# A table of score offsets kept in device memory as 128 copies of its strips instead of one, and read forwards instead of backwards

## The reference

```
bias_band = rel_bias[t5_bucket(dist[0])]                      # rel_bias: 32 buckets x 16 heads
s_band = einsum(q, k) * scale + bias_band
s_band = where((k_pos >= BLOCK) & (dist >= 0) & (dist < WINDOW), s_band, NEG)
bias_m = rel_bias[t5_bucket(dist_m)]                          # query against the 16 meta tokens
s_meta = where(dist_m >= 0, einsum(q, k_meta) * scale + bias_m, NEG)
p = softmax(concatenate([s_meta, s_band, sink]))
```

## Time and profile before

| | |
|---|---|
| median of 3 runs | 1749.38 us (1748.59 to 1753.09) |
| the profiled execution | 1753.09 us, its span 1751.3 us |
| PE busy | 1667.7 us, 95% of the span |
| DVE, ACT, POOL busy | 59%, 52%, 12% |
| bytes moved | 266.00 MB, of which POOL's queue 3.28 MB |
| TensorE clock granted | 0.986 of full speed on average |

### The profile page before, as it was taken

How to read it: one execution, slowest core, us unless ns; L and a number is a source line. 1 busy time by engine, 2 the same in 40 slices (tenths; PEclk the granted TensorE clock), 3 DMA queues, 4 the chain that set the end, 5 groups by cost and what they waited for, 6 DMA issues and landing times.

```text
span 1751.3 us, 31633 instructions
## 1 busy us (share of the span) xinstructions
PE 1667.7 (95%) x12915; PEld 1596.3 (91%) x12915; DVE 1033.4 (59%) x2139; ACT 911.5 (52%) x2008; POOL 217.5 (12%) x257
## 2 busy tenths in 40 slices
PE   8999999999999999999899997999977989999997
PEld 7999999899997999999889996988976769999997
DVE  5555566655555655554565554544366876768863
ACT  4444354644436544465465444566743447556653
POOL 4000000000000000001100000345433551200000
PEclk9999999999999999999999999999989999999999
DMA  8555535365554555643346554633351224645551
GB/s 276 175 169 175 182 125 172 122 190 169 177 178 131 169 179 180 194 131 114 121 144 190 177 187 120 176 113 104 113 154 60 78 69 136 201 145 177 179 181 43
DMA packets 260207, 266.00 MB, mean 152 GB/s; under 512 B 4755, under 2 KB 259025, under 8 KB 260064
## 3 DMA queue, kind: packets, MB, share of 16 engines
q1 hardware_dynamic: 258528, 260.72, 47.3%
q0 software_dynamic: 1536, 3.28, 0.8%
HBM read 262.89 MB, written 1.09 MB: 151 GB/s over the span
## 4 chain that ended last, share of the span: by engine, by line
PE 84%; issue 4%; ACT 4%; DVE 3%; POOL 3%; DMA 0%; SPq 0%; DVEq 0%; POOLq 0%; ACTq 0%
PE ps L803 51%; PE ps L805 25%; POOL EX L1911 2%; PE ps L516 1%; ACT wh L1137 1%; PE ps L772 1%; POOL YB L1939 1%; PE ps L615 1%; POOL EX L1912 0%; ACT H L918 0%; DVE BC L1684 0%; DVE wl L1626 0%; POOL wl L1947 0%; ACT XH L913 0%; PE ps L752 0%
## 5 line engine op out<-in xcount | busy, mean ns | idle before, releaser
L1626 DVE TENSOR_TENSOR wl<-raw,wh 128x512 fp32r<-128x512 f32 x923 | 609.9, 713 | 395.2 <-ACT wh L1137 386.7
L1137 ACT ACTIVATE wh<-raw 128x512 fp32r<-128x512 f32 (+1 forms) x989 | 548.2, 620 | 213.7 <-PE ps L803 212.9
L803 PE MATMUL ps<-XH,wh 128*128 128x272 f32 (+2 forms) x2264 | 577.5, 291 | 16.0 <-ACT XH L913 6.7
L805 PE MATMUL ps<-XH,wl 128*128 128x272 f32 (+2 forms) x2264 | 568.9, 287 | 0.0
L803 PEld LDWEIGHTS ps<-XH,wh 128*128 128x128 f32 x2264 | 431.2, 190 | 21.6 <-issue 14.7
L805 PEld LDWEIGHTS ps<-XH,wl 128*128 128x128 f32 x2264 | 432.5, 191 | 0.2
L803 PE MATMUL ps<-XL,wh 128*128 128x272 f32 (+2 forms) x2264 | 310.6, 288 | 0.2 <-DVE XL L1407 0.2
L803 PEld LDWEIGHTS ps<-XL,wh 128*128 128x128 f32 x2264 | 290.0, 189 | 4.2 <-DVE XL L1407 2.8
L803 PE MATMUL ps<-HH,wh 128*128 128x272 f32 (+1 forms) x704 | 173.1, 284 | 0.0
L805 PE MATMUL ps<-HH,wl 128*128 128x272 f32 (+1 forms) x704 | 173.1, 284 | 0.0
L803 PEld LDWEIGHTS ps<-HH,wh 128*128 128x128 f32 x704 | 132.5, 188 | 0.0
(11 more groups left out here) (363 smaller groups left out, 2022.2 us busy)
## 6 DMA issues: line engine op xcount, KB each, us to landing
raw<-in_ffn_wg SPq DMA_DIRECT2D x44, 1024.0 KB, 5.4
raw<-in_ffn_wu SPq DMA_DIRECT2D x44, 1024.0 KB, 5.4
raw<-in_w_in SPq DMA_DIRECT2D x33, 1024.0 KB, 5.4
raw<-in_ffn_wd SPq DMA_DIRECT2D x32, 1024.0 KB, 5.2
raw<-in_w_ffn_in SPq DMA_DIRECT2D x22, 1024.0 KB, 5.1
raw<-in_ffn_wd SPq DMA_DIRECT2D x16, 768.0 KB, 4.8
raw<-in_conv_w_in SPq DMA_DIRECT2D x12, 1024.0 KB, 5.1
raw<-in_kv_w SPq DMA_DIRECT2D x8, 1024.0 KB, 5.4
```

The source lines that it names most:

```text
L803: mm = e.matmul(o, hi[:, k, c], xk, start=u.first and part == 0 and k == 0, stop=u.last and end)
L805: e.matmul(o, lo[:, k, c], xk, start=False, stop=False)
L1137: e.activation(wh[u.n % NH][:, c], raw[u.n % NR][:, c], ACT.Copy).then_inc(s_hi, 1)
L1626: e.tensor_tensor(wl[u.n % NH][:, c], raw[u.n % NR][:, c], wh[u.n % NH][:, c].bitcast(F32), ALU.subtract).then_inc(s_lo, 1)
```

## The change

The scratch tensor grows from 16 x 672 numbers (43 KB) to 128 x 16 x 672 numbers (5.5 MB). One transfer still writes it, from the same 16 partitions, but its source is repeated 128 times, so each head's row of 2688 bytes is written 128 times, 43,008 bytes apart. The constants are built in the opposite order (the strips unreversed, and the strip of the window ahead of that of the meta tokens). The reads have the same shapes as before. Partition q now reads in copy q of the strips, at an offset that falls by 4 bytes from one q to the next; so the keys come out in rising order, and DVE adds the rows forwards. Number, order and shapes of all instructions on all engines stay as they were; the two parts of `B2` change places (16 and 256 columns).

```diff
-    db, dm = 255 - np.arange(STRIP)[::-1], 271 - np.arange(MSTRIP)[::-1]
-    both = np.concatenate([dm, db])
+    db, dm = 255 - np.arange(STRIP), 271 - np.arange(MSTRIP)
+    both = np.concatenate([db, dm])
...
-            e.tensor_tensor(SS[:, 0:272], PS[4][:, 0:T], B2[:, h, ::-1], ALU.add).then_inc(s_s2, 1)
+            e.tensor_tensor(SS[:, 0:272], PS[4][:, 0:T], B2[:, h, :], ALU.add).then_inc(s_s2, 1)
             e.wait_ge(s_sc1, 8 + h + 1)
-            e.tensor_tensor(SS[:, 272:288], PS[5][:, 0:16], B1[:, h, ::-1], ALU.add)
-            e.tensor_tensor(SS[:, 288:416], PS[5][:, 16:144], B2[:, h, 127::-1], ALU.add).then_inc(s_s1, 1)
-            e.tensor_tensor(SS[0:16, 416:432], PS[5][0:16, 144:160], B0[:, h, ::-1], ALU.add).then_inc(s_s0, 1)
+            e.tensor_tensor(SS[:, 272:288], PS[5][:, 0:16], B1[:, h, :], ALU.add)
+            e.tensor_tensor(SS[:, 288:416], PS[5][:, 16:144], B2[:, h, 144:272], ALU.add).then_inc(s_s1, 1)
+            e.tensor_tensor(SS[0:16, 416:432], PS[5][0:16, 144:160], B0[:, h, :], ALU.add).then_inc(s_s0, 1)
...
         e.wait_ge(s_smk, 1)
-        e.dma_start(scratch, SMK).then_inc(s_b, 16)
+        e.dma_start(scratch.rearrange("q h j -> h q j"),
+                    SMK.unsqueeze(1).to_broadcast([16, 128, WS])).then_inc(s_b, 16)
...
-        sk, sv = A["attn_sinks_2"], scratch
+        sk, sv, pitch = A["attn_sinks_2"], scratch, 16 * WS
 
         def shifted(off, nq, n):
-            return bass.AP(tensor=sv.tensor, offset=sv.offset + WS - n - off, ap=[[1, nq], [WS, 16], [1, n]])
+            return bass.AP(tensor=sv.tensor, offset=sv.offset + off, ap=[[pitch - 1, nq], [WS, 16], [1, n]])
...
-        e.dma_start(B2[:, :, 0:256], shifted(127, 128, 256)).then_inc(s_b, 16)
-        e.dma_start(B2[:, :, 256:272], shifted(STRIP + 271 - 144, 128, 16)).then_inc(s_b, 16)
+        e.dma_start(B2[:, :, 16:272], shifted(127, 128, 256)).then_inc(s_b, 16)
+        e.dma_start(B2[:, :, 0:16], shifted(STRIP + 271 - 144, 128, 16)).then_inc(s_b, 16)
...
-    scratch = nc.dram_tensor("strips", (16, STRIP + MSTRIP), F32, kind="Internal").ap()
+    scratch = nc.dram_tensor("strips", (128, 16, STRIP + MSTRIP), F32, kind="Internal").ap()
```

More of the change, by code:

```diff
@@ L43, in bucket @@
         return np.where(d < 16, d, np.minimum(big, 31))
-    db, dm = 255 - np.arange(STRIP)[::-1], 271 - np.arange(MSTRIP)[::-1]
-    both = np.concatenate([dm, db])
+    db, dm = 255 - np.arange(STRIP), 271 - np.arange(MSTRIP)
+    both = np.concatenate([db, dm])
     hot = (bucket(both)[None, :] == np.arange(32)[:, None]).astype(np.float32)
-    ok = np.concatenate([dm >= 0, (db >= 0) & (db < 128)])
+    ok = np.concatenate([(db >= 0) & (db < 128), dm >= 0])
     smask = np.broadcast_to(np.where(ok, 0.0, NEG).astype(np.float32), (16, both.size))
```

## The result

| | before | after |
|---|---|---|
| median | 1750.17 us (4 runs, 1748.59 to 1753.09) | 1780.51 us (4 runs, 1778.31 to 1784.07) |
| the profiled execution | 1753.09 us, span 1751.3 | 1777.53 us, span 1775.7 |
| POOL's queue | 3.28 MB | 8.74 MB |

The ratio is 1.018, with a 95% interval of 1.0164 to 1.0198 (it goes by all 21 executions of the changed kernel, the table's median by four of them): some 30 us slower. The forecast was 1771, in a range of 1748 to 1784.

The account below looks back on a forecast made before the run. The prediction took PE to bound the kernel around the write, with weights 24 us ahead; 19.2 us for late weights plus 2.0 for the clock, 21.2 on the median of 1749.38, gave 1771 us, range 1748 to 1784.

Parts of the forecast that it names:

- What bounds, and the lead: Around the strips' write PE has no gap, 634 to 694 us; the weight stream runs 24 us ahead of it.
- G: Gate weight unit SP issues at 636.88, after the write; PE late only if it lands after 666.1; forecast to land at 668.
- as long as the write less 24 us: Sign during the write: if PE's gap has this length, the mechanism stands even if the write took another time.
- The rate of the source: The 5.5 MB write from 16 partitions goes at 101 GB/s, taking 54.5 us, from 635.7 to 690.2.
- What the weights get: During the write: some 5 us without any, then one 1 KB packet per row; PE 19.2 us late.
- U: Up weight unit SP issues at 642.80; forecast to land near 691, with PE starting on it at 692.2 instead of 673.0.
- The clock: After PE's standstill of some 17 us, a granted clock of 0.50 costs 2.0 us; bounds 0 and 3.
- The wait of the residual: DVE's first residual waits for the write to land; it moves to about 715, so the write is in time, no cost.
- The reads: POOL's reads from 1100 us, same shapes with addresses 43 KB apart: taken as 0, bounds 0 and up to 12 us.
- a rival allowed: Rival: reads get faster without 128 partitions reading one 43 KB copy; at most 1 us, 1748; 0.02 for over 5 us.
- a hidden write: Rival: the 16 partitions don't limit the write, so both weight units land in time; 1749 to 1752 us, chance 0.31.
- weights that pass it: Rival: the write is slow, but engines fetch weights while a row's source keeps them waiting; 1749 us, chance 0.06.

## Why the prediction was right, and where it wasn't

- **What bounds, and the lead.** Right. G was to be needed at 666.1, with the stage's shift of 0.89 at 667.0. It landed at 693.2, 26.2 us late, and the gap is 26.6. With half the bytes it landed at 668.0, 1.9 us late, and the gap is 2.3. Two numbers beside it were wrong. A write of 36 us as the point where the loss begins: one of 30.5 us already had a gap. And the sign "as long as the write less 24 us": that is 32.7, not 26.6, since G is issued 2.1 us after the write and takes 5.4 us in any case. It comes out in G's landing time: 55.4 - 5.4 - 24 = 26.0.
- **The rate of the source.** Right: 101 GB/s was taken from a 0.4 us window, and the write ended at 692.3 where 690.2 was forecast. Since the window holds little (15 records of 2688 bytes, not all 16 rows), that it came out so near is partly luck. The 0.21 us a row of the same group, by which the write would have been hidden, was misleading: it was taken with one row for each engine, and over the whole write an engine needs 56.7/128 = 0.44 us for a row.
- **What the weights get.** Right in kind, mis-sized. The prediction took a row for a packet, and 5 us without any weights. It was two rows, and some 15 us without any. So G, forecast at 668, landed at 693, and it is G that PE waited for, not U. The term was 19.2, measured 26.6, too small by 7.4 us. The case that the prediction named beside its sum ("if the weights got nothing at all", 27 us) has nearly the number, but it isn't what happened: 0.72 MB of weights passed up to 690, and the write ended 2.1 us later and G landed 0.9 us behind it instead of 3.1. The trace of before could have told both. In the earlier trace rows 0.77 MB in 198 packets is four rows of 1 KB each, so a packet isn't a row. And from 1100 to 1108 POOL's queue had passed 355 packets, 1.33 MB, before the weights got their first.
- **The clock.** Right: in the window 695:700, at 0.50, PE issues 25 matmuls for 44, which is 2.2 us lost; it had started at 694.74, and the gap leaves 2.6 of the 29.2 us. Forecast 2.0.
- **The sum and the range.** 21.2 us were forecast, 26.6 + 2.6 = 29.2 arose. The measured 1780.51 lies within 1748 to 1784, but the upper end stood for something else, a write of 68 us. The write was as forecast, and the late weights took the time up there.
- **The wait of the residual.** Never met: DVE's first residual came at 724.30, 32 us after the write.
- **The reads.** They got faster, which a rival allowed: 10.7 us instead of 13.3. In 2 us in which POOL's queue is alone it moves 0.72 MB (1134:1136 of the kernel after) instead of 0.47. No gain can be told from it, as that rival's own bound of 1 us said: the run with 128 source partitions has these reads and no gap, at a ratio of 0.9993 (0.9977 to 1.0009).
- **DVE's forward reads.** 438 ns for 437. Nothing.
- **The rivals.** Those of a hidden write and of weights that pass it fell, by the gap. The first comes true with 128 source partitions: 19.1 us, no gap.

No version beats the kernel before: the changed kernel with the write from 128 partitions is level with it.

## What to carry to other kernels

Before adding a transfer beside a prefetch stream, work out two numbers: how long the transfer keeps the DMA engines (its bytes over what its narrow side allows, here 106 GB/s for 16 partitions against 400 for 128), and how far ahead the stream is. Measure it at the landing of the first load that is issued behind the transfer: in every run with the write on POOL's queue this load landed after the write's end, by 3 us at most. Weights that were late by less than the lead cost nothing here, beyond it each us was paid in full. Spreading the source over 128 partitions hid all of the 30 us (ratio 0.9993). Half the bytes from 16 partitions still cost 4 us in its trace, too little for the times to tell. The transfer cut in two cost 12 us, as the second piece ran into the end of the layer; at a better place it might cost less, which wasn't tried. A side that repeats rows ought to be spread over 128 partitions first.

## What the runs showed of the hardware that was not expected

- A later load gets nothing while the other queue moves its first 1.3 to 1.6 MB, whether that takes 5 us or 16. POOL's queue had passed about 284 packets by 652 in the changed kernel (16 us), 319 with half the bytes (16 us), 299 by 645 with 32 partitions (8 us) and 301 by 641 in the changed kernel with 128 source partitions (5 us): 18 to 20 for each engine, 1.5 to 1.6 MB. The reads of the kernel before had passed 355 by 1108, 1.33 MB. But ACT's queue had passed 566 of one row by 650, 1.52 MB, so it isn't the number of packets that these have in common. Why it is so wasn't tried.
- A gap of 2.3 us in PE was followed by a lower clock, part of the window at 0.50: 670:675 of the run with half the bytes has PE busy all the time at a mean of 0.66. After the gaps of 1.9 and 1.5 us, with 32 and 64 partitions, the same window has 1.00.

```profile
665.00:670.00 5.00, 2.74 (x23) 2.56 (x22) 1.25 (x3) 1.92 (x4) 0.00 (x0) 1.00 1.10 361
670.00:675.00 5.00, 5.00 (x32) 5.00 (x31) 4.41 (x9) 3.38 (x9) 0.00 (x0) 0.66 1.10 349
```

- 128 partitions that read overlapping rows out of one 43 KB region got 0.47 MB in 2 us, 235 GB/s; the same rows out of separate copies 0.72 MB, 360 GB/s, although in both the start moves by 4 bytes within a copy from one partition to the next. That the overlap is the cause is the plain reading, but no run changed it alone.
